# Layer 0's convolution: four of sixteen channel blocks on GpSimd, VectorE's running sums in PSUM

## What is computed

```python
def _conformer_conv(h, w_in, b_in, w_dw, b_dw, ln_g, ln_b, w_out, b_out):
    a, gate = jnp.split(h @ w_in + b_in, 2, axis=-1)
    u = a * jax.nn.sigmoid(gate)
    u = lax.conv_general_dilated(
        u, w_dw[:, None, :], window_strides=(1,),
        padding=[(CONV_WIDTH - 1, 0)],
        dimension_numbers=('NWC', 'WIO', 'NWC'),
        feature_group_count=D_MODEL) + b_dw
    u = jax.nn.silu(_layernorm(u, ln_g, ln_b))
    return u @ w_out + b_out
```

## Time and profile before

| what | value |
|---|---|
| median of 3 runs | 3117.28 us (3116.04 to 3117.61) |
| profiled execution | 3116.24 us, its span 3114.5 us |
| busy: TensorE | 2886.3 us, 93% of the span |
| busy: VectorE | 2304.6 us, 74% |
| busy: GpSimd | 1503.4 us, 48% |
| busy: ScalarE | 537.9 us, 17% |
| VectorE's multiply-adds of the convolution (L1489) | 480, 191.1 us busy |
| mean granted TensorE clock | 0.977 of full speed |

### The profile page before, as it was taken

The page is one execution under the profiler, slowest core; times in us unless marked ns, Lnnn a source line. Parts: engine busy times, 40 slices in busy tenths (PEclk is TensorE's granted clock), DMA queues, the critical chain, the costliest instruction groups (busy, mean ns, idle before and its releaser), DMA issues. The chain is left out here.

```text
span 3114.5 us, 45255 instructions
## 1 busy us (share of the span) xinstructions
PE 2886.3 (93%) x12838; PEld 2076.5 (67%) x12838; DVE 2304.6 (74%) x4886; ACT 537.9 (17%) x1365; POOL 1503.4 (48%) x1567
## 2 busy tenths in 40 slices
PE   7988988999999999999899988869999999999997
PEld 5766867677777655565588857767777776655564
DVE  3999799888888866766432754998888888666766
ACT  2123216100000000000322152152000000000001
POOL 0001463555555677777200361544555555777773
PEclk9998989999999999999999999989999999999999
DMA  8553543899999999999643322336999999999997
GB/s 331 222 204 138 187 180 121 351 410 401 410 407 405 404 410 410 410 409 410 229 145 112 136 68 81 116 115 269 410 407 407 402 408 405 410 410 410 410 410 304
DMA packets 242632, 956.16 MB, mean 307 GB/s; under 512 B 26937, under 2 KB 27113, under 8 KB 224874
## 3 DMA queue, kind: packets, MB, share of 16 engines
q0 software_dynamic: 147456, 536.94, 43.8%
q1 hardware_dynamic: 95082, 418.12, 34.8%
HBM read 952.85 MB, written 2.10 MB: 307 GB/s over the span
## 5 line engine op out<-in xcount | busy, mean ns | idle before, releaser
L960 PE MATMUL out_e<-weights,mod_rows 128*128 128x512 f32 x2048 | 933.8, 599 | 65.6 <-DVE mod_rows L1727 63.7
L951 PE MATMUL acc<-h_t,weights 128*128 128x256 f32 x4096 | 930.6, 380 | 0.0
L951 PEld LDWEIGHTS acc<-h_t,weights 128*128 128x128 f32 x4096 | 781.0, 191 | 218.3 <-issue 124.5
L507 POOL DMA_INDIRECT v_rows<-in_pk_v,idx_now x512 | 636.0, 1242 | 572.5 <-DVE mod_rows L1665 449.9
L1665 DVE SCALAR_TENSOR_TENSOR mod_rows<-v_rows,dots_acts,mod_rows 128x1024 f32<-128x1024 f32 x512 | 657.8, 1285 | 186.5 <-DMA v_rows<-in_pk_v,idx_now 184.3
L960 PEld LDWEIGHTS out_e<-weights,mod_rows 128*128 128x128 f32 x2048 | 377.9, 190 | 472.3 <-issue 369.3
L1648 DVE SCALAR_TENSOR_TENSOR u_rows<-u_rows,h_rows 128x1024 f32<-128x1024 f32 x512 | 625.8, 1222 | 83.2 <-DMA u_rows<-in_pk_u,idx_now 81.9
L501 POOL DMA_INDIRECT u_rows<-in_pk_u,idx_now x512 | 572.5, 1118 | 236.0 <-issue 144.9
L540 POOL CAST top_f<-top_i 128x64 f32<-128x64 uint32 x32 | 7.6, 236 | 702.9 <-DVEq L1606 694.7
L1329 ACT ACTIVATE mod_rows<-acc 128x256 f32<-128x256 f32 x256 | 96.2, 383 | 1204.1 <-PE acc L951 1200.7
L1727 DVE TENSOR_TENSOR mod_rows<-mod_rows,region 128x256 f32<-128x256 f32 x256 | 109.6, 428 | 200.8 <-ACT mod_rows L1329 197.2
(11 more groups left out here) (250 smaller groups left out, 2339.2 us busy)
## 6 DMA issues: line engine op xcount, KB each, us to landing
weights<-in_u_t SPq DMA_DIRECT2D x256, 512.0 KB
weights<-in_pk_v SPq DMA_DIRECT2D x256, 512.0 KB, 6.7
weights<-in_pk SPq DMA_DIRECT2D x32, 1024.0 KB, 4.8
v_rows<-in_ada SPq DMA_DIRECT2D x30, 1024.0 KB, 6.9
weights<-in_w_qkv SPq DMA_DIRECT2D x24, 1024.0 KB, 4.8
weights<-in_w_in SPq DMA_DIRECT2D x16, 1024.0 KB, 7.7
weights<-in_ada SPq DMA_DIRECT2D x8, 1024.0 KB, 4.8
weights<-in_w_out SPq DMA_DIRECT2D x8, 1024.0 KB, 4.9
```

The costliest lines, as they stand in the source:

```text
L507: nc.gpsimd.indirect_dma_start(v_rows[:, r % VR, :], None, a["pk_v"], bass.IndirectOffsetOnAxis(ap=idx_now[:, 1, par, r:r + 1], axis=0)).t ...
L951: last = nc.tensor.matmul(acc[s][:, 0:HALF], weights[:, s, k * P:(k + 1) * P], h_t[:, k, :], start=k == 0, stop=k == KB - 1)
L960: last = nc.tensor.matmul(out_e[2 * tt + c][:, :], e_act[:, s, tt * P:(tt + 1) * P], weights[:, s, D + c * 512:D + (c + 1) * 512], start=F ...
```

## The change

Twelve blocks stay on VectorE: in the first half the pair (0,1), block 2 alone, the pairs (4,5) and (6,7); in the second half block 3 alone and the pairs (4,5) and (6,7). GpSimd takes (0,3), (1,0), (1,1) and (1,2) in that order, ahead of its first table. Each of its taps is a product into one of three scratch slices of `region` (`products`) and an addition to the running sum in `c_ts[h]`, in SBUF; the product of the next tap is issued ahead of the addition. Before a block it waits for the block's gate, and in the second half for VectorE to have gated the same block of the first half, whose last columns it reads.

VectorE's running sums go to `sum_of`, the two halves of the bank `out_e[2]`; the last tap writes `c_ts[h]`. A pair has one half bank for each block. A single block sums its even taps in the one and its odd taps in the other and adds them at the end. For this the mean and the variance share the bank `out_e[1]`, so `variance` waits for both centrings. `means` waits for VectorE's blocks and for GpSimd's by two semaphores, and VectorE waits for GpSimd's block (0,3) before it works on (1,3). The residuals of the first half stand after 4, 14, 24 and 31 taps of the last pair.

```diff
--- before.py
+++ after.py
@@ -280,8 +280,13 @@
 
         first_banks = [mid, [acc[1], out_e[3]]]
         first_turned = [out_e[2:4], acc]
-        mean, var = out_e[1][:, 0:HALF], out_e[2][:, 0:HALF]
-        mean_part, var_part = out_e[1][:, HALF:2 * HALF], out_e[2][:, HALF:2 * HALF]
+        mean = var = out_e[1][:, 0:HALF]
+        mean_part = var_part = out_e[1][:, HALF:2 * HALF]
+
+        sum_of = [out_e[2][:, i * HALF:(i + 1) * HALF] for i in range(2)]
+        products = [region[:, at:at + HALF] for at in (9728, 9984, 12288)]
+
+        POOL_BLOCKS = ((0, 3), (1, 0), (1, 1), (1, 2))
 
         def col(name, i=None, n=1):
             at, size = COLS[name]
@@ -310,6 +315,7 @@
         found, looked_up, best_ready, exp_ready, picks_ready = map(
             sem, ("found", "looked_up", "best_ready", "exp_ready", "picks_ready"))
         masked = sem("masked")
+        pad_ready, pool_conv_ready = sem("pad_ready"), sem("pool_conv_ready")
         part_full, part_ready = sem("part_full"), sem("part_ready")
         iota_ready = sem("iota_ready")
         z_full, sigs_ready, a_ready, a_t_full, a_t_ready, o_full, o_ready = map(
@@ -529,6 +535,33 @@
                 nc.gpsimd.iota(iota_places, pattern=[[1, TOPK], [0, 4 * TOPK]], base=0, channel_multiplier=0,
                                allow_small_or_imprecise_dtypes=True).then_inc(iota_ready, 1)
 
+            def convolve(n):
+
+                h, k = POOL_BLOCKS[n]
+                pool.wait_ge(acc_free, free("glu", 0, h, k))
+                if h:
+
+                    pool.wait_ge(conv_ready, k // 2 + 1)
+                to = c_ts[h][:, k, :]
+                now = u_t[:, k, PAST + h * HALF:PAST + (h + 1) * HALF]
+
+                def product(j):
+                    steps.behind(nc.gpsimd.tensor_scalar(products[j % 3], u_t[:, k, h * HALF + j:h * HALF + j + HALF],
+                                                         col("w_dw", k * WIDTH + j), None, ALU.mult))
+
+                steps(nc.gpsimd.tensor_tensor(now, now, to, ALU.mult))
+                steps.behind(nc.gpsimd.tensor_scalar(to, u_t[:, k, h * HALF:h * HALF + HALF], col("w_dw", k * WIDTH),
+                                                     col("b_dw", k), ALU.mult, ALU.add))
+                product(1)
+                for j in range(1, WIDTH):
+                    if j + 1 < WIDTH:
+                        product(j + 1)
+                    else:
+                        steps.settle()
+                    steps.behind(nc.gpsimd.tensor_tensor(to, to, products[j % 3], ALU.add))
+                steps.settle()
+                pool.sem_inc(pool_conv_ready, 1)
+
             def look_up(l, h, head):
 
                 number = PK[l, h] + head
@@ -567,6 +600,11 @@
                                                            pattern=[[-1, P]], channel_multiplier=1)
                         last.then_inc(masked, 1)
 
+            pool.wait_ge(pad_ready, 1)
+            pool.wait_ge(cols_in, 16)
+            for n in range(len(POOL_BLOCKS)):
+                convolve(n)
+
             for q in range(2 * DEPTH):
                 if q % 2 == 0:
                     l = q // 2
@@ -696,7 +734,14 @@
 
             def means(h, pairs):
                 for i in pairs:
-                    pe.wait_ge(conv_ready, h * (KB // 2) + i + 1)
+                    if h + i:
+
+                        pe.wait_ge(conv_ready, h * (KB // 2) + i + 1 - h)
+                    else:
+                        pe.wait_ge(conv_ready, 1)
+                    mine = [n for n, (half, k) in enumerate(POOL_BLOCKS) if half == h and k // 2 == i]
+                    if mine:
+                        pe.wait_ge(pool_conv_ready, mine[-1] + 1)
                     for k in (2 * i, 2 * i + 1):
                         last = in_strip(mean_part, c_ts[h], k)
                 if i == KB // 2 - 1:
@@ -709,6 +754,7 @@
                                         stop=k >= KB - STRIPS, tile_position=(0, at))
 
             def variance(h):
+                pe.wait_ge(centred, 2 * h + 2)
                 for k in range(KB):
                     if k % (KB // 2) == 0:
                         pe.wait_ge(squared, 2 * h + k // (KB // 2) + 1)
@@ -1471,23 +1517,34 @@
                 tt_op(to, to, both, ALU.add).then_inc(acc_free, 1)
                 dve.wait_ge(acc_free, free("out", l, h, i))
 
-            def conv(h, i, taps):
+            def conv(h, blocks, taps):
 
                 if taps[0] == 0:
-                    for k in (2 * i, 2 * i + 1):
+                    for k in blocks:
                         dve.wait_ge(acc_free, free("glu", 0, h, k))
-                    now = u_t[:, 2 * i:2 * i + 2, PAST + h * HALF:PAST + (h + 1) * HALF]
-                    steps(tt_op(now, now, c_ts[h][:, 2 * i:2 * i + 2, :], ALU.mult))
+                        if (0, k) in POOL_BLOCKS:
+
+                            dve.wait_ge(pool_conv_ready, POOL_BLOCKS.index((0, k)) + 1)
+                    both = slice(blocks[0], blocks[-1] + 1)
+                    now = u_t[:, both, PAST + h * HALF:PAST + (h + 1) * HALF]
+                    steps(tt_op(now, now, c_ts[h][:, both, :], ALU.mult))
                 for j in taps:
-                    for k in (2 * i, 2 * i + 1):
-                        to = c_ts[h][:, k, :]
+                    for k in blocks:
+                        sums = sum_of[k % 2 if len(blocks) > 1 else j % 2]
+                        to = c_ts[h][:, k, :] if j == WIDTH - 1 else sums
                         seen = u_t[:, k, h * HALF + j:h * HALF + j + HALF]
                         tap = col("w_dw", k * WIDTH + j)
                         if j == 0:
-                            steps.behind(ts_op(to, seen, tap, col("b_dw", k), ALU.mult, ALU.add))
+                            step = ts_op(to, seen, tap, col("b_dw", k), ALU.mult, ALU.add)
+                        elif j == 1 and len(blocks) == 1:
+                            step = ts_op(to, seen, tap, None, ALU.mult)
                         else:
-                            steps.behind(stt_op(out=to, in0=seen, scalar=tap, in1=to, op0=ALU.mult, op1=ALU.add))
+                            step = stt_op(out=to, in0=seen, scalar=tap, in1=sums, op0=ALU.mult, op1=ALU.add)
+                        steps.behind(step)
                 steps.settle()
+                if len(blocks) == 1:
+
+                    steps(tt_op(to, to, sum_of[1], ALU.add))
                 if taps[-1] == WIDTH - 1:
                     dve.sem_inc(conv_ready, 1)
 
@@ -1774,7 +1831,8 @@
             nc.vector.tensor_reduce(strips[:, :], ident[:, :].rearrange("p (j m) -> p m j", j=STRIPS), axis=AX.X, op=ALU.add
                                     ).then_inc(strips_ready, 1)
             reciprocal_root(0, 0, 0)
-            steps(nc.vector.memset(u_t[:, :, 0:PAST], 0.0))
+            nc.vector.memset(u_t[:, :, 0:PAST], 0.0).then_inc(pad_ready, 1)
+            dve.wait_ge(pad_ready, 1)
             spread_columns(0)
             dve.wait_ge(mod_ready, 1)
             dve.wait_ge(xn_t_full, 4)
@@ -1785,27 +1843,25 @@
             reciprocal_root(0, 1, 0)
 
             every = range(WIDTH)
-            conv(0, 0, every)
-            conv(0, 1, every)
-            conv(0, 2, every)
-            conv(0, 3, every)
-            conv(1, 0, range(0, 15))
+            conv(0, (0, 1), every)
+            conv(0, (2,), every)
+            conv(0, (4, 5), every)
+            conv(0, (6, 7), every)
+            conv(1, (3,), every)
             spread_columns(1)
             centre(0)
-            conv(1, 0, range(15, WIDTH))
+            conv(1, (4, 5), range(0, 15))
             normalise(0)
-            conv(1, 1, range(0, 20))
+            conv(1, (4, 5), range(15, WIDTH))
+            conv(1, (6, 7), range(0, 4))
             residual(0, 0, 0)
-            conv(1, 1, range(20, WIDTH))
+            conv(1, (6, 7), range(4, 14))
             residual(0, 0, 1)
-            conv(1, 2, range(0, 10))
+            conv(1, (6, 7), range(14, 24))
             residual(0, 0, 2)
-            conv(1, 2, range(10, 20))
+            conv(1, (6, 7), range(24, WIDTH))
             residual(0, 0, 3)
-            conv(1, 2, range(20, 25))
             reciprocal_root(0, 0, 1)
-            conv(1, 2, range(25, WIDTH))
-            conv(1, 3, every)
             rank(0, 0, 0)
             centre(1)
             rank(0, 0, 1)
```

## The result

The changed kernel is slower: 3130.94 us against 3116.72 on the same chip (medians of six runs each), a ratio of 1.0046 with a 95% interval of 1.0033 to 1.0059. Its profiled execution took 3127.71 us, span 3126.0, 11.5 us more than the one of before. It is the quickest of the six; the medians differ by 14.2 us, and what follows accounts for the 11.5.

The account below looks back on a forecast made before the run. VectorE's queue, delaying the fourth residual and so TensorE's transposes, was taken as the bound. VectorE's course, -1.0 us, plus contention, 3.1, gave +2.1 on the median 3117.3: 3119 us, range 3112 to 3136.

Parts of the forecast that it names:

- a dearer tap: Rival on VectorE's multiply-adds into PSUM: up to 80 ns more each, 21 us on top, 3140 us; chance 0.18.
- the second rival: GpSimd late before the second half's means: block 58 us, TensorE stands 34 us, 3151 us; chance 0.05.
- Prize at most 9.2 us, the rest hidden: Before the transposes, 9.2 of TensorE's 14.4 us idle are VectorE's; its other freed work, behind 240 us, is hidden.
- the first bound: VectorE's convolution taps queued ahead of the fourth residual, holding TensorE's transposes back by 9.2 us.
- A tap in PSUM at 0.397 us: VectorE's multiply-adds with sums in PSUM start 0.397 us apart, as before; bounds 0.03 less, 0.08 more.
- a cheaper tap: Rival on VectorE's taps: 0.367 us each and GpSimd hardly disturbing, 3108 to 3112 us; chance 0.09.
- VectorE's course: VectorE's new queue up to the fourth residual: 9 us idle before 100.5, ending at 233.6 against 234.54, 1 us sooner.
- The new wait for SiLU: Normalisation starts at 184.4 instead of 182.32, so SiLU ends later and leaves TensorE 1.2 us late, which it can bear.
- Contention 3.1 us: GpSimd lengthens VectorE's two-input SBUF instructions after 153 us: seven by 0.4 each, the normalising pair by 0.32.
- the rival in which contention is not removed: 155 VectorE taps from 153 us on wait some 0.3 us each for GpSimd, 46 us: 3165 us; chance 0.04.
- "Costed at nothing": GpSimd's four blocks, at 1.1 to 1.3 us a tap, end at 231 to 249, before TensorE needs them at 269.00.
- The rival's own threshold: GpSimd delays TensorE at the second half's means from 1.52 us a tap, 46.7 us a block; chance 0.05.

## Why the prediction was right, and where it was wrong

The measured 3130.9 us lies in the range, but that is luck: the likeliest case, no change (3119 us, 2.1 over the kernel before), did not come, and the range reached up to 3136 for a dearer tap that did not come either. What came was the second rival, given 0.05 and priced at 3151 us; it cost 14.2 us over the kernel before.

- **Prize at most 9.2 us, the rest hidden.** True for the first bound. The early residuals alone showed that it is worth nothing without an earlier end of the convolution; with both, about 11 us.
- **A tap in PSUM at 0.397 us.** Right: 0.393, with and without GpSimd. The rivals of a dearer and of a cheaper tap (0.18 and 0.09) have nothing for them. The Trainium skill's "Perfetto Trace Analysis", on optimizing ScalarE and VectorE operations, gives some 60 ns of access on SBUF and 125 on PSUM; the difference of 65 ns shows here neither in the reads nor in the taps that also write there. Tap 0 at 0.544 us is 0.13 dearer, as taken.
- **VectorE's course.** Right in the main: idle 9.53 us where 9 were given, the reciprocal of the normalising starts at 183.06 - 50.90 = 132.2 us behind the first gating product, where 184.4 less 52.3 is 132.1. Without contention the path to residual 3 is 182.1 - 2.1 = 180.0 us, 2.2 less than before where 1.0 was given. The new wait for SiLU left TensorE 1.52 us late where 1.2 were given, and it bore it.
- **Contention 3.1 us.** Measured on the seven instructions and the pair: 0.37 + 0.46 + 0.19 for the gating products, 0.53 for the pair, 0.07 + 0.09 + 0.37 for the additions, 2.1 us. Mis-sized, within its bounds. So the prediction's -1.0 + 3.1 = +2.1 us at the fourth residual came out as -2.2 + 2.1 = -0.1. That the multiply-adds would be spared was right: 482 ns busy against 479, and 662 with the sums in SBUF, so the rival in which contention is not removed (0.04) is out. The Trainium skill's rule in "SBUF — State Buffer", on who interferes with whom, is that a VectorE instruction with at most one SBUF input, outside the two-port modes, does not contend with GpSimd, and one with two does if GpSimd reads SBUF; both figures agree.
- **"Costed at nothing": the step that failed.** This is GpSimd's share, for which the prediction's sum has no term, and it was worth the whole loss. The product was priced at 0.43 to 0.62 us from a copy of 64 elements, the dear end being two nanoseconds an element; it took 0.935. The addition, priced from bf16, took 0.73 for 0.667. A tap is 1.60 us, not 1.1 to 1.3, a block 49.7 to 51.2, not 34 to 40. The rival's own threshold, 1.52 us a tap or 46.7 a block, was right: three blocks of some 50.4 overrun the cover by 3 x (50.4 - 46.7) = 11.1 us, and the trace shows 10.86 (GpSimd's start, 127.1 for 129, and the means, 267.6 for 269, are both earlier, and nearly cancel). The cause that the rival named, contention lengthening GpSimd, was wrong: a tap takes 1.60 us also from 91 to 99 us, while VectorE is idle, and the other form of the product alone made it 1.24.

The chance of 0.05 was the weak point. The bound of 1.3 us a tap stood 15% under the threshold, and it came from rows of another operation, size and type.

## What to carry to other kernels

Work moved to an idle engine is not free because the engine is idle: its price must come from the same operation, form, size and type, and where no row has it, the distance to the deadline must be weighed as a risk of its own. Where two bounds stand close behind each other, moving one alone shows nothing: here, against the kernel before, early residuals alone gave 0, an earlier end of the convolution alone (three blocks on GpSimd) gave 0, and both together gave 0.34%. A faster instruction on a second engine can take back part of its gain on the first: the shorter product removed a wait of 10.9 us, and the ratio fell only from 1.0046 to 1.0025.

## What the runs showed of the hardware

- GpSimd's multiplication of 256 f32 elements by a column took 0.935 us on average in the one-operation form and 0.602 (0.55 at its shortest) in the form that also adds a column. Why is not known here.
- VectorE's multiply-add with its sum in PSUM: every 0.393 us, written and read back, with GpSimd busy or idle, against 0.397 in SBUF with GpSimd idle. With the sum in SBUF and GpSimd busy it was itself busy for 0.662 us, against 0.482 in PSUM. Tap 0, a product and an addition of a column, went from 0.410 to 0.544 us when it wrote to PSUM.
- Two-input additions of 512 f32 elements in SBUF on VectorE, 0.69 us alone, took up to 1.06 us in the first half's residuals beside GpSimd's long taps and up to 1.70 beside its short ones. The residuals' products, which have one of their two inputs in PSUM, took 0.69 us beside either.
